# Four stage boundaries of a three-block transformer kernel: small tables, a partial sum, a normalisation and gate operands move into neighbouring stages

## The reference

```python
# second block: feed-forward, with modulation vectors computed from a condition c (rms norm, shift, squared relu)
h = rmsnorm(x, gain) * (1 + scale) + shift
x = x + gate * ((relu(h @ w_ff_in) ** 2) @ w_ff_out)
# third block
h = rmsnorm(x, norm_mix_g)
proj = h @ w_in           # mq, mk, mv, mo, mi, mf, dq, dk, dv, gates
...                       # mLSTM over mq, mk, mv with the gates mi, mf; its output times sigmoid(mo)
a = probs(q1, k1) - lam * probs(q2, k2)      # differential attention, 4 heads, causal, softmax in blocks of 128 queries
hd = head_rmsnorm(a @ v) * (1 - lam_init)
mixed = sigmoid(g_a) * (hm @ w_br_m) + sigmoid(g_b) * (hd @ w_br_d)
x = x + mixed @ w_out
```

## Time and profile before

| what | value |
|---|---|
| median of 3 runs | 3627.01 us (3626.55 to 3630.5) |
| the profiled execution's own time | 3628.23 us |
| its span, from the first to the last instruction | 3626.4 us |
| mean granted PE clock | 0.96 of full |
| PE busy | 3333.6 us (92%) |
| DVE busy | 2040.0 us (56%) |
| ACT busy | 940.6 us (26%) |
| POOL busy | 462.1 us (13%) |

### The profile page before, as it was taken

How to read it: one execution, slowest core, us unless ns; L and a number is a source line. 1 busy time by engine, 2 the same in 40 slices (tenths; PEclk the granted TensorE clock), 3 DMA queues, 4 the chain that set the end, 5 groups by cost and what they waited for, 6 DMA issues and landing times. The chain is left out here.

```text
span 3626.4 us, 50871 instructions
## 1 busy us (share of the span) xinstructions
PE 3333.6 (92%) x21218; PEld 2721.2 (75%) x21218; DVE 2040.0 (56%) x2756; ACT 940.6 (26%) x1662; POOL 462.1 (13%) x363
## 2 busy tenths in 40 slices
PE   7889999999899999899969889899989779899998
PEld 6678788878778877688748777687868568688786
DVE  6455644444464454699856663434446565688744
ACT  2036300111342241223253440222020460100104
POOL 0000111000013552100024430000020000100001
PEclk9899999999999999999989999999999889999998
DMA  3111122232304553332200003222222202322221
GB/s 131 50 54 48 47 93 93 79 108 90 87 28 159 186 174 112 103 110 94 73 28 4 3 4 116 70 93 93 93 71 93 96 1 82 104 93 93 73 96 70
DMA packets 210403, 298.62 MB, mean 82 GB/s; under 512 B 32802, under 2 KB 111278, under 8 KB 210062
## 3 DMA queue, kind: packets, MB, share of 16 engines
q1 hardware_dynamic: 210190, 295.59, 24.4%
HBM read 291.25 MB, written 4.32 MB: 82 GB/s over the span
## 5 line engine op out<-in xcount | busy, mean ns | idle before, releaser
L447 PE MATMUL bank<-h_hi_cut,ring_hi_cut 128*128 128x512 f32 x1960 | 774.9, 395 | 60.8 <-DVE h_cut L538 15.9
L447 PE MATMUL bank<-h_hi_cut,ring_cut 128*128 128x512 f32 x1960 | 768.2, 392 | 0.0
L447 PE MATMUL bank<-h_cut,ring_hi_cut 128*128 128x512 f32 x1864 | 731.5, 392 | 0.0
L500 DVE CAST ring_hi_cut<-ring 128x4096 fp32r<-128x4096 f32 (+3 forms) x97 | 197.7, 2038 | 641.0 <-DMA ring<-in_ffn_w_gu 138.6
L447 PEld LDWEIGHTS bank<-h_hi_cut,ring_hi_cut 128*128 128x128 f32 x1960 | 371.1, 189 | 145.9 <-issue 42.9
L447 PEld LDWEIGHTS bank<-h_hi_cut,ring_cut 128*128 128x128 f32 x1960 | 370.7, 189 | 79.9
L447 PEld LDWEIGHTS bank<-h_cut,ring_hi_cut 128*128 128x128 f32 x1864 | 353.0, 189 | 76.0 <-issue 2.2
L502 DVE TENSOR_TENSOR ring_cut<-ring,ring_hi_cut 128x4096 fp32r<-128x4096 f32 (+3 forms) x97 | 380.6, 3923 | 7.6 <-issue 0.4
L447 PE MATMUL bank<-hidden_cut,ring_hi_cut 128*128 128x512 f32 x848 | 324.9, 395 | 0.0
L447 PEld LDWEIGHTS bank<-hidden_cut,ring_hi_cut 128*128 128x128 f32 x848 | 159.9, 189 | 40.1 <-issue 1.2
L332 POOL TENSOR_TENSOR work<-work 128x512 f32<-128x512 f32 x35 | 52.7, 1507 | 1003.6 <-ACT work L316 1003.4
(11 more groups left out here) (606 smaller groups left out, 5909.1 us busy)
## 6 DMA issues: line engine op xcount, KB each, us to landing
ring<-in_ffn_w_gu SPq DMA_DIRECT2D x44, 1024.0 KB, 6.5
ring<-in_w_in SPq DMA_DIRECT2D x21, 2048.0 KB, 7.8
ada_w<-in_ada_w SPq DMA_DIRECT2D x12, 2048.0 KB, 8.0
ring<-in_w_up SPq DMA_DIRECT2D x22, 1024.0 KB, 6.8
ring<-in_w_ff_in SPq DMA_DIRECT2D x8, 2048.0 KB, 8.6
ring<-in_w_ff_out SPq DMA_DIRECT2D x8, 2048.0 KB, 8.0
ring<-in_ffn_w_down SPq DMA_DIRECT2D x8, 1536.0 KB, 6.6
ring<-in_w_out SPq DMA_DIRECT2D x6, 2048.0 KB, 7.9
```

The lines of the kernel that those rows point to most:

```text
L447: last = nc.tensor.matmul(to, lhs, rhs, start=st and q == 0, stop=sp_ and q == len(parts) - 1)
L500: dve.tensor_copy(high, whole)
```

## The change

A. `norm` is gone. In `g_out2`, ACT now squares each new tile of `x` and also writes `h = gain * x`, POOL adds the squares, and PE sums them in `pe_tail`. `r_row` is now rms itself, not its inverse; the tile that is projected is `gain * x + rms * shift`, that is rms times the old `h`, made in one DVE instruction a tile (`add_shift`) inside `g_ff_in`. Its first slab runs over the k tiles in the outer loop and over the four output tiles in the inner one. The result is multiplied by 1/rms squared (`square_factor`, `add_result`: two DVE instructions a tile instead of one).

B. The memsets and the four transfers move into `g_in3`.

C. The gate operands (8 ACT copies, 8 DVE subtractions) and the cut of the first gate slab (8 ACT copies and 8 DVE subtractions of 512 columns) move into the third block's attention, two kinds in turn: pairs 0 and 1 make the operands, pairs 2 and 3 cut the slab. The sum and root of `s_one` move into `heads_to_channels`. The attention's buffers move to make room (`homes`, `at`, the slot of `band`).

D. `add_up` of part 9 moves from the end of `g_gu` to the start of `g_down`.

```diff
@@ project
+                if shape and i is None and j == 0:
+                    for k in range(nk):
+                        pe.wait_ge(cut_acts.sem, cut_acts.done(k))
+                        for m in range(4):
+                            wc = slice(m * P, (m + 1) * P)
+                            for q, (p_w, p_a) in enumerate(((w_hi[:, k, wc], hi[k]), (w_hi[:, k, wc], lo[k]), (w[:, k, wc], hi[k]))):
+                                last = nc.tensor.matmul(bank[m][:], p_w, p_a, start=k == 0 and q == 0, stop=k == nk - 1 and q == 2)
...
+                    if shape and j == 0:
+                        for k in range(2):
+                            shape(dve, k).then_inc(shaped.sem, 1)
                     for k in range(k0, k0 + nk):
...
+                            if shape and k + 2 < nk:
+                                shape(dve, k + 2).then_inc(shaped.sem, 1)
@@ gated_ffn
                 def gu_pool(pool, j):
                     rescale(pool, j)
-                    if j >= 1:
+                    if 1 <= j < GU - 1:
                         add_up(pool, j - 1)
...
                 def down_pool(pool, j):
+                    if j == 0:
+                        add_up(pool, GU - 2)
                     if j <= 1:
                         add_up(pool, GU - 1 + j)
@@ second block
+                def squares_on_act(act):
+                    for k in range(DT):
+                        act.wait_ge(dve_took.sem, dve_took.done(k))
+                        if k >= 3:
+                            act.wait_ge(tail_sum.sem, tail_sum.done(k - 3))
+                        act.activation(work[:, k % 2, :] if k else sqsum, x[:, k, :], ACT.Square).then_inc(tail_sq.sem, 1)
+                        act.activation(h[:, k, :], x[:, k, :], ACT.Copy, scale=gain_f[:, k:k + 1])
+                        if k == DT - 2:
+                            act.activation(r_col[:, 0:1], eps[:, 0:1], ACT.Sqrt)
+                    act.wait_ge(summed.sem, summed.done(0))
+                    act.activation(r_row, bank[0][:], ACT.Sqrt, bias=eps[:, 0:1], scale=1.0 / D)
...
+                def squares_on_pe(pe):
+                    pe.wait_ge(dve_took.sem, dve_took.done(0))
+                    pe.wait_ge(tail_sum.sem, tail_sum.done(DT - 3))
+                    nc.tensor.matmul(bank[0][:], ones, sqsum, start=True, stop=False)
+                    pe.wait_ge(tail_sq.sem, tail_sq.done(DT - 1))
+                    nc.tensor.matmul(bank[0][:], ones, work[:, (DT - 1) % 2, :], start=False, stop=True).then_inc(summed.sem, 1)
...
-            norm(x, DT, lambda k: gain_f[:, k:k + 1], h, shift=lambda k: mod[:, 24 + k:25 + k])
+                def add_shift(dve, k):
+                    last = dve.scalar_tensor_tensor(h[:, k, :], r_row, mod[:, 24 + k:25 + k], h[:, k, :], ALU.mult, ALU.add)
+                    if k == DT - 1:
+                        dve.tensor_copy(s_one[:], r_row)
+                    return last
+
+                def square_factor(dve):
+                    dve.reciprocal(r_square, s_one[:])
+                    dve.drain()
+                    dve.tensor_tensor(r_square, r_square, r_square, ALU.mult)
+                    dve.drain()
+
+                def add_result(dve, j, m, ps, n, s):
+                    dve.scalar_tensor_tensor(ps[:], ps[:], mod[:, 40 + n:41 + n], r_square, ALU.mult, ALU.mult)
+                    dve.drain()
+                    return dve.tensor_tensor(x[:, n, :], ps[:], x[:, n, :], ALU.add)
@@ third block, front
+                    def small_loads(sp):
+                        sp.dma_start(b_if[:], a["b_if_t"]).then_inc(loaded.sem, 16)
+                        sp.dma_start(tri[:], a["c_causal_band"][:, 3 * P:4 * P]).then_inc(loaded.sem, 16)
+                        sp.wait_ge(consts_made.sem, consts_made.done(0))
+                        for n, c in enumerate((0, 32)):
+                            sp.dma_start(wg[:, :, c:c + MH], w3[:, 2048 + n * MH:2048 + (n + 1) * MH].rearrange("(k p) c -> p k c", p=P)).then_inc(loaded.sem, 16)
...
                     def store_rows(sp, j):
+                        if j == 1:
+                            small_loads(sp)
@@ third block, attention
+                        k = i * 4 + u - 3
+                        if 3 <= u < 7 and k < DT:
+                            act.activation(h_hi[:, k, :], x[:, k, :], ACT.Copy, scale=gain3(k)).then_inc(tail_hi.sem, 1)
+                        elif 3 <= u < 7:
+                            part = eighths[k - DT]
+                            if k == DT:
+                                act.wait_ge(weights_here[gate_slot].sem, weights_here[gate_slot].done(0))
+                            act.activation(ring_hi[:, gate_slot, part], ring[:, gate_slot, part], ACT.Copy).then_inc(early_hi.sem, 1)
+
+                    def gate_operands(dve, i, u):
+                        k = i * 4 + u - 4
+                        if 4 <= u < 8 and k < DT:
+                            tail_on_dve(dve, k, gain3)
+                        elif 4 <= u < 8:
+                            part = eighths[k - DT]
+                            dve.wait_ge(early_hi.sem, early_hi.done(k - DT))
+                            last = dve.tensor_tensor(ring_cut[:, gate_slot, part], ring[:, gate_slot, part], ring_hi[:, gate_slot, part].bitcast(F32), ALU.subtract)
+                            if k == 2 * DT - 1:
+                                last.then_inc(cut.sem, 1)
```

More of the change, by code:

```diff
@@ L697, in project @@
                 t.advance(up_to[n])
[L700 to L742, removed]
-            squared.advance(n)
-            summed.advance(1)
-            rooted.advance(1)
-            if tail:
-                dve_took.advance(n)
-                tail_over(tail)
         def tok_to_ch(src, tiles, take, extra_act=None):
@@ L1445, in _, with heads_to_channels @@
                             pool.drain().then_inc(en["sum"].sem, 1)
-        def heads_to_channels(t, ss, factor, take, first=None, then=None):
+        def heads_to_channels(t, ss, factor, take, first=None, then=None, pe_first=None):
             with nc.Block() as block:
@@ new lines, in squares_on_pool @@
+                def squares_on_pool(pool):
+                    pool.wait_ge(tail_sq.sem, tail_sq.done(0))
+                    for k in range(1, DT - 1):
+                        pool.wait_ge(tail_sq.sem, tail_sq.done(k))
+                        pool.tensor_tensor(sqsum, sqsum, work[:, k % 2, :], ALU.add)
+                        pool.drain().then_inc(tail_sum.sem, 1)
+                def squares_on_pe(pe):
[4 more added lines that the diff above has]
+                    nc.tensor.matmul(bank[0][:], ones, work[:, (DT - 1) % 2, :], start=False, stop=True).then_inc(summed.sem, 1)
@@ L3230, in head_squares, with sum_final, root_final @@
                                 square_sum(act, o_tok[:, t, c * P:(c + 1) * P], ss[:, t * 4 + c:t * 4 + c + 1], dump[:])
+                        k = i * 4 + u - 3
[16 more added lines that the diff above has]
+                                last.then_inc(cut.sem, 1)
+                    def sum_final(pe):
+                        nc.tensor.matmul(bank[4][:], ones, s_one[:], start=True, stop=True).then_inc(summed.sem, 1)
+                    def root_final(eng):
+                        if eng is nc.scalar:
+                            eng.wait_ge(summed.sem, summed.done(0))
+                            eng.activation(s_one[:], bank[4][:], ACT.Sqrt, bias=eps[:, 0:1], scale=1.0 / D)
                     def subtract(dve, i, u, ps, r):
@@ L3252, in gate3 @@
                     act.activation(gates[:, j * 4 + m, :], gates[:, j * 4 + m, :], ACT.Sigmoid).then_inc(gated.sem, 1)
-            with nc.Block() as block:
-                @block.tensor
-                def _(pe):
-                    nc.tensor.matmul(bank[7][:], ones, s_one[:], start=True, stop=True).then_inc(summed.sem, 1)
-                @block.scalar
-                def _(act):
-                    for k in range(DT):
-                        act.activation(h_hi[:, k, :], x[:, k, :], ACT.Copy, scale=gain3(k)).then_inc(tail_hi.sem, 1)
-                    act.wait_ge(summed.sem, summed.done(0))
-                    act.activation(s_one[:], bank[7][:], ACT.Sqrt, bias=eps[:, 0:1], scale=1.0 / D)
-                @block.vector
-                def _(dve):
-                    for k in range(DT):
-                        tail_on_dve(dve, k, gain3)
-            summed.advance(1)
-            tail_hi.advance(DT)
             def final_x(dve, j):
```

67 lines of the change are left out of this document (45 added, 22 removed).

## The result

| | median of 5 runs | range |
|---|---|---|
| before, on the same chip | 3626.55 us | 3625.15 to 3630.5 |
| changed kernel | 3606.51 us | 3602.11 to 3609.99 |

The ratio is 0.9943, with a 95% interval of 0.9929 to 0.9958: faster by 20 us, where I had forecast 36 and a range that ended at 3601. The trace of the changed kernel tells at each boundary what became of the terms.

A forecast was written before the change was run, and what follows sets the result against it. PE, busy 92% of the span, bounds the kernel, so time is won only in its waits. 18.9 + 3.6 + 6.6 + 7.1 = 36.2 us off 3628.2 gives 3592.0, or 3590.8 on the median's scale; range 3582 to 3601.

The forecast's parts named there:

- D: End of g_gu and g_down: moving part 9's additions wins 7.1 us, bounds 5 and 7.8.
- So up to 1.4 us of wait; I take 0.7: In g_down: PE's wait for part 11, ready at 1390 to 1391.7 us and asked for at 1390.3.
- one such addition: In g_down: one POOL addition slowed beside DVE's cut costs 4.2 us more, making D 2.9 instead of 7.1.
- C: Third attention and behind heads_to_channels: 12.8 us gone, pairs grow 6.2, net 6.6 us won, bounds 2.8 to 10.8.
- A and B: Start of g_ff_in: 18.9 us won, bounds 17 to 20.7; start of g_in3: 3.6 us won, bounds 2.5 and 5.1.
- The new loop order: First slab of g_ff_in: DVE delivers a tile each 1.3 us, PE takes 2.5 us for one, so PE stays fed.
- a wait for the last `reduce` over 1.5 us: In g_down: PE's wait for the last reduce was to be under 1.5 us.
- part 11 later than slab 3: In g_down: sign that the forecast is wrong, if part 11 comes later than slab 3.
- No pair went over 16 us: Third attention: pairs were to take 14 to 15 us; over 16 us would show the forecast wrong.
- slab 0 of `g_ff_in` had no gaps: Start of g_ff_in: gaps in PE's work on slab 0 would show the forecast wrong.
- the low end: Low end of the total with unknown costs at their bounds: 3580.5 us, from gains of 44.4; also written as 3582.6.
- not 51: Third attention, rival that the kernel gets slower: the attention would have to grow 42 us on 51; chance 1%.

The follow-up runs named there:

- e2: The kernel before with only part 9's addition moved from the end of g_gu to the start of g_down; 3633.44 us, ratio 1.0019.
- e5: Changed kernel, g_down asking for the last two parts' sums a slab later, part 11's transfer issued behind slab 3's load; 3595.07 us, ratio 0.9914.
- e10: e5 with part 9's first two additions done ahead of the meeting point at the end of g_gu; 3590.11 us, ratio 0.9894.
- e7: Changed kernel with D undone, ACT's copies kept in the attention, DVE's subtractions moved behind heads_to_channels; 3608.47 us, ratio 0.9947.
- e12: e5 with the first slab of g_ff_in again running over the four output tiles in the outer loop; 3599.51 us, ratio 0.992.
- e1: Changed kernel with D undone, part 9 added up at the end of g_gu again; 3601.24 us, ratio 0.9928.

## Why the prediction was wrong

- **D is the step that failed**, and nearly all of the error: -7.7 instead of +7.1, 14.8 of the 16.3 us between 36.2 and the 19.9 that the stretches give. In the prediction's words: "So up to 1.4 us of wait; I take 0.7". I had the row for it (5.48 us against 1.26) and worked out 2.9 us by "one such addition". It isn't one. The eighteen L2186 additions behind the meeting took 2.0 us in the mean against 1.29, 12.8 us more in all, since each part now runs beside a slab's cut and the tiles' cuts behind it; and the two transfers took 9.1 and 8.4 us from issue to ACT's first multiplication (1354.01 to 1363.12, 1378.77 to 1387.13) where I had 8.0. From the end of one part's additions to the end of the next it took 24.8 and 24.0 us where I had 19.4. Part 11 was ready at 1402.7, not 1390 to 1391.7, and PE waited for part 10 too, which I had put at nothing. Waits and clock lost 3.99 + 7.37 + 1.7 + 1.8 = 14.9 us against some 7.6 won at the meeting (6.1 of waiting, 1.5 of clock). e2 shows the cost without the other edits, e5 and e10 that it lies in the waits.
- That mechanism got no rival and no chance of its own, though it spoke against the change, and even its own 2.9 lies outside the bounds I gave D, 5 to 7.8. The overlap could have been read from the trace: POOL's ends and DVE's casts were 0.5 and 6 us apart before.
- **C:** the mechanism was right, the growth of the pairs mis-sized, 9.6 instead of 6.2. I had counted ACT's 2.5 and 2.1 us a pair only; ACT's share came out at 5.1 where I had 6.2, and DVE's, which I put at nothing, at 4.2 (e7). The clock gave 1.8 back.
- **A and B** were right, 18.8 and 3.7 us for 18.9 and 3.6. The new loop order does keep PE fed, as forecast; the 5.4 us that I expected from undoing it came out at 1.3 to 2.2 (e12).
- Two signs that I had named came out against me: a wait for the last `reduce` over 1.5 us, part 11 later than slab 3. No pair went over 16 us, and slab 0 of `g_ff_in` had no gaps.
- Two figures of my working don't come out of its sums: the low end is 3582.6, as it says beside it, and not 3580.5; and the four pairs took 49.1 us, not 51. Neither moves the forecast or saves the range.

## What to carry to other kernels

Before work is moved past a meeting point, lay the timelines of the two engines beside each other for the whole chain that hangs on it, not for the first link: here an engine was as fast as alone only while the other rested. Where a chain of transfers and sums feeds PE, ask first whether PE can ask later; here that was worth more than speeding up the chain. And count the extras of every engine in a loop: DVE was busy for 9.9 of 12.9 us in a pair without extras, and its own extras still lengthened the four pairs by 4.2 us.

## What the runs showed of the hardware

POOL and DVE hold each other up instruction by instruction, in both directions. An addition of 128x512 takes 1.29 us alone, 2.0 in the mean beside DVE's cuts; DVE's difference of 128x512 takes 0.68 alone and up to 1.78 beside an addition. I hadn't expected copies with one input to take part.

PE's granted clock over the 3.55 us behind a wait was 1.00 after waits of 1.20 and 1.55 us, and 0.50 to 0.53 after 3.99, 7.37 and 7.72 us. In between, equal waits went either way. After 3.31 us at A it began high and fell in the changed kernel (0.70 over 3.55 us), and was 0.50 from the first product in e5. After 1.64 us, ahead of the sum of `s_one`, the two products ran at 0.50 in the changed kernel and at 1.00 in e1.
